# Two unused gaps ahead of the activation tiles in a decoder layer kernel

## The reference

```
h = rmsnorm(x) * (1 + sc_a) + sh_a
proj = h @ w_in                       # 1024 x (512+512+1024+1024+16+6*1024)
o_a, o_b = chunked gated linear attention, 4 heads and 8 heads
merged = sigmoid(ma) * rmsnorm(o_a) * silu(gg) + sigmoid(mb) * rmsnorm(o_b) * silu(hg)
x = x + g_a * (merged @ w_out)        # 1024 x 1024
h = rmsnorm(x) * (1 + sc_f) + sh_f
u = causal conv of width 3 over (h @ w_up) + conv_b       # 1024 x 5632
x = x + g_f * ((silu(gate) * up) @ w_down)                # 2816 x 1024
out = rmsnorm(x)
```

## Time and profile before

| | us |
|---|---|
| median of 3 timed runs | 872.92 |
| lowest and highest of them | 872.38, 873.68 |
| profiled execution, span from first to last instruction | 872.24 |
| TensorE busy in it | 857.7 |
| VectorE busy | 607.5 |
| ScalarE busy | 488.0 |
| GpSimd busy | 252.5 |

### The profile page before, as it was taken

The page is one execution under the profiler, slowest core; times in us unless marked ns, Lnnn a source line. Parts: engine busy times, 40 slices in busy tenths (PEclk is TensorE's granted clock), DMA queues, the critical chain, the costliest instruction groups (busy, mean ns, idle before and its releaser), DMA issues.

```text
span 872.2 us, 12717 instructions
## 1 busy us (share of the span) xinstructions
PE 857.7 (98%) x4688; PEld 710.6 (81%) x4688; DVE 607.5 (70%) x779; ACT 488.0 (56%) x739; POOL 252.5 (29%) x227
## 2 busy tenths in 40 slices
PE   7999999999999999999999999999999999999997
PEld 6778888887888888888887888888888888888885
DVE  3598988678867867774955466744444444599995
ACT  4576556577557657756756443633333333356574
POOL 2123779624122230330444000211111111534200
PEclk9999999999999999999999999999999999999999
DMA  9997497283644546455225931533333336599912
GB/s 336 354 320 130 118 209 103 74 237 112 174 145 131 146 124 178 116 163 162 79 74 181 157 97 49 145 96 96 96 96 96 96 96 228 112 270 206 233 36 97
DMA packets 149235, 130.21 MB, mean 149 GB/s; under 512 B 4743, under 2 KB 132065, under 8 KB 148928
## 3 DMA queue, kind: packets, MB, share of 16 engines
q1 hardware_dynamic: 136048, 110.84, 42.2%
q0 software_dynamic: 13136, 18.69, 12.7%
HBM read 125.31 MB, written 4.20 MB: 148 GB/s over the span
## 4 chain that ended last, share of the span: by engine, by line
PE 73%; ACT 2%; DVE 1%; POOL 0%; issue 0%; POOLq 0%
PE ps L2220 17%; PE ps L2222 17%; PE ps L2221 17%; PE ps L2653 4%; PE ps L2651 4%; PE ps L2652 4%; PE ps L2387 1%; PE ps L2542 1%; PE ps L2543 1%; PE ps L2546 1%; PE ps L2389 1%; PE ps L2367 1%; PE ps L2351 1%; PE ps L2354 1%; PE ps L2399 0%
## 5 line engine op out<-in xcount | busy, mean ns | idle before, releaser
L2220 PE MATMUL ps<-h_hi,w_hi 128*128 128x512 f32 (+1 forms) x568 | 223.3, 393 | 0.4 <-DVE w_lo L1852 0.4
L2222 PE MATMUL ps<-h_lo,w_hi 128*128 128x512 f32 (+1 forms) x568 | 219.5, 386 | 0.0
L2221 PE MATMUL ps<-h_hi,w_lo 128*128 128x512 f32 (+1 forms) x568 | 219.4, 386 | 0.0
L2220 PEld LDWEIGHTS ps<-h_hi,w_hi 128*128 128x128 f32 x568 | 106.7, 188 | 22.9 <-issue 1.0
L2221 PEld LDWEIGHTS ps<-h_hi,w_lo 128*128 128x128 f32 x568 | 106.7, 188 | 22.3 <-issue 1.0
L2222 PEld LDWEIGHTS ps<-h_lo,w_hi 128*128 128x128 f32 x568 | 106.7, 188 | 21.7
L983 POOL TENSOR_TENSOR prod<-conv 128x512 f32 x21 | 43.3, 2062 | 219.3 <-DVE conv L2062 219.3
L1384 ACT ACTIVATE conv<-ps,vecs 128x512 f32<-128x512 f32 x42 | 32.6, 778 | 132.3 <-PE ps L2222 123.9
L2058 DVE SCALAR_TENSOR_TENSOR conv<-ps,vecs,conv 128x511 f32<-128x511 f32 x44 | 33.0, 749 | 104.8 <-ACT conv L1384 102.5
L1852 DVE TENSOR_TENSOR w_lo<-raw,w_hi 128x1024 fp32r<-128x1024 f32 x46 | 58.1, 1275 | 56.1 <-ACT w_hi L1025 56.0
L1511 DVE TENSOR_TENSOR w_lo<-raw,w_hi 128x1024 fp32r<-128x1024 f32 x52 | 63.9, 1232 | 1.3 <-ACT w_hi L1017 1.2
(11 more groups left out here) (312 smaller groups left out, 1819.1 us busy)
## 6 DMA issues: line engine op xcount, KB each, us to landing
raw<-in_w_in_dram SPq DMA_DIRECT2D x44, 512.0 KB, 4.0
raw<-in_w_up_dram SPq DMA_DIRECT2D x44, 512.0 KB, 3.9
ada_w<-in_w_ada_dram SPq DMA_DIRECT2D x32, 512.0 KB, 4.5
ada_w<-in_w_ada_dram SPq DMA_DIRECT2D x8, 1024.0 KB, 9.3
g_blocks<-in_w_in_dram SPq DMA_DIRECT2D x24, 256.0 KB, 6.2
hres<-in_w_down_dram POOLq DMA_DIRECT2D x12, 512.0 KB, 8.8
raw<-in_w_down_dram SPq DMA_DIRECT2D x11, 512.0 KB, 5.1
raw<-in_w_out_dram SPq DMA_DIRECT2D x8, 512.0 KB, 5.6
```

What stands on the lines that cost most here:

```text
L2220: pe.matmul(dst, a_hi, b_hi, start=start and i == 0, stop=False)
L2221: pe.matmul(dst, a_lo, b_hi, start=False, stop=False)
L2222: last = pe.matmul(dst, a_hi, b_lo, start=False, stop=stop and i == n - 1)
```

## The change

Two tensors that nothing reads or writes are declared, one ahead of `h_hi` (16 float32, 64 bytes in each partition) and one ahead of `h_lo` (48 float32, 192 bytes). With them `h_hi` starts 64 bytes and `h_lo` 256 bytes past a multiple of 512, while `raw`, `w_hi` and `w_lo` stay at a multiple of 512, and all that is declared behind `h_lo` lies 256 bytes further on. No instruction is added, removed or put elsewhere.

```diff
         raw = sb("raw", [P, RAW, KT, P])
         w_hi = sb("w_hi", [P, RING, KT, P], F32R)
         w_lo = sb("w_lo", [P, RING, KT, P], F32R)
+        h_hi_start = sb("h_hi_start", [P, 16])
         h_hi = sb("h_hi", [P, KT, T], F32R)
+        h_lo_start = sb("h_lo_start", [P, 48])
         h_lo = sb("h_lo", [P, KT, T], F32R)
         vecs = sb("vecs", [P, 3 * P])
```

## The result

The changed kernel takes 890.07 us (median of 4 runs, 889.28 to 891.12) against 873.3 before: ratio 1.0196, 95% interval 1.0183 to 1.0208. The forecast was 860.0 with a range of 849 to 885. What came is the time of rival 1, at the price of its upper end (890).

What follows compares the result with a forecast made beforehand. The pace of TensorE's 512-column float32r matmuls (226.7 ns each) was taken as the bound. Span 872.2 less 12.7 and 0.2 gives 859.3, plus 0.7 for timed runs: 860.0 us, range 849 to 885.

Steps and rivals of the forecast that it cites:

- rival 1: Matmuls with h tiles: the new distances are worse, up to +17.1 us (890), centre about 881; chance 0.37.
- part (b): Everything behind h_lo moves by 256 bytes; 300 comb and p0 matmuls go from distance 128 to 384; taken as 0.
- the bound of 17.1: Worst case for the 2946 matmuls with h tiles: 232.5 ns spacing, +5.8 ns each, +17.1 us in all.
- comb's price: Matmuls with comb tiles as weights, at distance 128: 232.5 ns from start to start, 5.8 more than with h tiles.
- part (a): h_hi at 64 and h_lo at 256 from the weights: 2946 matmuls gain 4.3 ns each, 12.7 us.
- 218 ns as a bound: Best case for matmuls with h tiles: excess of the half-rate plain float32 matmuls, -8.7 ns each, -25.6 us.
- Rival 2: Matmuls with h tiles: nothing happens, the 13.3 ns excess is a fixed step; 872.9 within 1.7 us; chance 0.14.
- Rival 3: All matmuls of the threes: excess falls to that of the half-rate matmuls, -25.6 us, 847.3; chance 0.08.
- the 32 us: Estimate by the skill page's 215.7 ns if the excess goes entirely: 2946 x 11 ns less, about 840.5.

## Why the prediction was wrong

**Right.** That nothing but the pace of the float32r matmuls could move the end; the counts; that the first stage and the feeding engines take no part (the first value matmul starts at 21.88 us, 21.85 before); part (b), 0 within the interval (only what stands behind h moved: 1.0001). That the loss of 17.2 us of span falls on the bound of 17.1, all 2946 matmuls at comb's price, is luck: 1506 of them, in the up and down stages, lost 6.7 ns each, those of the block stage about 5.3 (227.3 to 232.6), and the distances are others than comb's.

**The step that failed** is the value in part (a), "a gain of half the better distance, -4.3 ns". It measured +6.7 ns in the up and down stages (233.3 against 226.7), and 17.2 us / 2946 = +5.8 ns on average: 17.2 us lost where 12.7 were to be gained. Of its two reasons one was wrong and the other led nowhere.

- "At distance 0 load and stream start together in the same place ... the most crowded arrangement". With 128 loaded and 512 streamed columns, as in this kernel, no place tried is better than distance 0: 65 places in steps of 4 bytes, and 58 mixtures, gave nothing below 226.7 ns.
- "It comes, at least in part, with a load beside a stream at full rate". The comparison with plain float32 showed a difference between kinds of matmul, and I read it as a difference in crowding that distance could relieve, with 218 ns as a bound. A load of 32 columns has no less excess. bfloat16 has 215.9 ns with the same number of columns and a load beside it, but it also moves half the bytes, so crowding by the rate of the stream is neither shown nor ruled out. What is shown is that no distance tried comes near the bound.

The rows had the sign in them. They showed two distances, 0 and 128, and the one that wasn't 0 was slower; the even 389 at distance 0 beside 395 at 128 was written into rival 1. I set an untested picture of the memory against the only measured slope, and gave it 0.41 to 0.37.

**The rivals.** Rival 1 came, and the first half of its mechanism holds: at distance 0 the matmuls go at a steady 226.7, and the change breaks this pace (228, 237, 235 in turn after). Evenness in itself is not what makes it fast: at 132 bytes the spacing is an even 240. Its centre of 881 and its prices of 5.7 and 11.4 us added up one price per matmul by distance; in fact 256 costs nothing, and 64 in two of three matmuls costs all 17, the third at distance 0 being slowed with them. Rival 2's rule, the Trainium skill, "SBUF — State Buffer", section "Who interferes with whom", that TensorE's two read ports are independent and it never waits, does not describe float32r here: the spacing moves between 226.7 and 240.0 ns when nothing but the place of the stream changes. It does agree with bfloat16, which had 216 ns at three distances. Rival 3's bound has no distance that reaches it. The other page named, the Trainium skill, "TensorE: Matmul & The Clock Gate", section "Wait — 56ns, not 53.3ns?", with 215.7 ns for 512 columns, is right for bfloat16 (215.9 measured) and 11 ns short for float32r; of the 32 us that an estimate by it put within reach, none of the places tried here brings any.

**What stays open.** Why some distances fall into step and others don't. The up stage with h as stream had 233.3 ns, a block with the stream always at 64 had 228.9, one of threes with a single load tile 231.1, and one with two load tiles 233.3 in the kernel's pattern, so what the matmuls just before did enters as well. Even a constant distance has no single value: stream at 128 had 233.3 in two runs and, behind other blocks, 232.4 in a third. Whether the excess comes with the float32r kind or with the rate of its stream was not separated. And open is the slower first stage when all small tiles move by 64 or 128 bytes.

## What to carry to other kernels

Before moving a tile, look in the trace for another tile that already stands where it would go, and believe that slope before any picture of the memory; here comb at 128 told the sign. Of all the places tried here, float32r matmuls with 128 loaded and 512 streamed columns were nowhere faster than with both operands at the same place modulo 256 bytes (with 64 loaded columns they were): keep big tiles in multiples of that, and check the tiles behind odd-sized small ones (`ada`, `fss` and `lbt`, 192 + 32 + 160 = 384 bytes, had pushed comb and p0 off by 128). Pace shows in the distance of starts, and a change of a group's mean duration by a few ns between two kernels (389 to 395) is worth following up there when the groups have thousands of members together.

## What the runs showed of the hardware that I had not expected

- float32r matmuls of 512 columns at 2.4 GHz never came closer than 226.7 ns on a block's average, bfloat16 ones had 215.9; the excess over the stream does not shrink with the number of loaded columns (32: 231.5 ns), but which distance is best changes with it.
- The spacing depends on the distance of the two operands, sign included, from 226.7 (0, 28, 60, 108, 156, 252 bytes) to 240.0 ns (132, 196, 244), and repeated after 256 bytes, though not after 64 or 128.
- Constant spacings of float32r matmuls are multiples of 6.67 ns (120.0, 173.3, 226.7, 233.3, 240.0), and where they vary, the sum over the repeating pattern was one in those looked at (686.7 for three at stream 64, 700 for the kernel's three, 1626.7 for seven with the load at 128).
- Matmuls at different distances are not priced one by one: in threes at 64, 64 and 0 the one at 0 is slowed too (700 ns for three).
- With fewer streamed columns the time does not always fall: 500, 504 and 512 columns all have 226.7 ns, 488 had 225.7 and 492 only 220.0.
